# Weight tiles interleaved by columns with a step per stage, and two banks taken in turn, in a two-layer decoder trunk

## The reference, cut to what matters

```python
h = h + 0.5 * swiglu(rmsnorm(h, ffn1_norm[l]), ffn1_w_in[l], ffn1_w_out[l])
u = rmsnorm(h, mix_norm[l])
q_a, c_kv, iq, ik, iw, z_pool, q_c, gate_pre = jnp.split(u @ w_in[l], split_pts, axis=-1)
...
y_c = mem_attention(q_c, rmsnorm(mem, mem_norm[l]), w_mem_kv[l])
g = jax.nn.sigmoid(gate_pre).reshape(B, S, N_BRANCH, D)
merged = (g[:, :, 0] * (y_a @ w_branch_a[l])
          + g[:, :, 1] * (y_b @ w_branch_b[l])
          + g[:, :, 2] * (y_c @ w_branch_c[l]))
h = h + merged @ w_out[l]
h = h + 0.5 * swiglu(rmsnorm(h, ffn2_norm[l]), ffn2_w_in[l], ffn2_w_out[l])
```

## Time and profile before

| | |
|---|---|
| median of 3 runs | 2218.6 us (2218.0 to 2218.61) |
| the profiled execution's own time | 2218.74 us |
| its span in the trace | 2216.8 us |
| PE matmuls | 10264, busy 2200.5 us (99%) |
| PE weight loads | 10264, busy 1805.8 us (81%) |
| POOL busy | 1327.2 us (60%) |
| DVE busy | 932.4 us (42%) |
| ACT busy | 521.8 us (24%) |
| transfers | 209.72 MB, mean 95 GB/s |

### The profile page before, as it was taken

How to read it: one execution, slowest core, us unless ns; L and a number is a source line. 1 busy time by engine, 2 the same in 40 slices (tenths; PEclk the granted TensorE clock), 3 DMA queues, 4 the chain that set the end, 5 groups by cost and what they waited for, 6 DMA issues and landing times.

```text
span 2216.8 us, 30470 instructions
## 1 busy us (share of the span) xinstructions
PE 2200.5 (99%) x10264; PEld 1805.8 (81%) x10264; DVE 932.4 (42%) x1697; ACT 521.8 (24%) x1010; POOL 1327.2 (60%) x886
## 2 busy tenths in 40 slices
PE   9999999999999999999999999999999999999997
PEld 6888888878888888888888888887878888888886
DVE  5331345578854432023433213536887453320322
ACT  3110112443553211001111101125445432100111
POOL 7656657644446666665766666585444376656654
PEclk9999999999999999999999999999999999999999
DMA  5343323322213332332333332242222132323322
GB/s 185 95 138 103 101 76 115 104 67 63 71 53 101 96 101 82 104 100 86 96 109 126 105 106 95 81 129 85 63 72 67 48 114 95 95 88 106 100 76 85
DMA packets 68780, 209.72 MB, mean 95 GB/s; under 512 B 7600, under 2 KB 10840, under 8 KB 68440
## 3 DMA queue, kind: packets, MB, share of 16 engines
q1 hardware_dynamic: 64416, 203.10, 29.6%
q10 hardware_dynamic: 4280, 5.52, 0.8%
HBM read 206.48 MB, written 3.68 MB: 95 GB/s over the span
## 4 chain that ended last, share of the span: by engine, by line
PE 96%; DVE 2%; DMA 0%; issue 0%; ACT 0%; ACTq 0%; DVEq 0%
PE bank L613 30%; PE bank L614 29%; PE bank L615 29%; PE obank L866 2%; PE sbank L811 1%; PE tbank L833 1%; DMA h<-in_xT 0%; PE sbank L803 0%; DVE picks L1384 0%; PE sbank L764 0%; PE sbank L786 0%; PE sbank L817 0%; PE obank L850 0%; PE obank L624 0%; DVE top L1382 0%
## 5 line engine op out<-in xcount | busy, mean ns | idle before, releaser
L544 POOL TENSOR_TENSOR wL<-raw,wH 128x1024 fp32r<-128x1024 f32 (+3 forms) x424 | 894.2, 2109 | 35.4
L541 POOL TENSOR_SCALAR wH<-raw 128x1024 fp32r<-128x1024 f32 (+3 forms) x424 | 398.2, 939 | 818.6 <-PE bank L615 795.5
L613 PE MATMUL bank<-u0H,wH 128*128 128x512 f32 x1376 | 537.4, 391 | 0.0
L615 PE MATMUL bank<-u0L,wH 128*128 128x512 f32 x1376 | 535.4, 389 | 0.0
L614 PE MATMUL bank<-u0H,wL 128*128 128x512 f32 x1376 | 535.3, 389 | 0.0
L614 PEld LDWEIGHTS bank<-u0H,wL 128*128 128x128 f32 x1376 | 258.3, 188 | 54.5 <-issue 1.0
L613 PEld LDWEIGHTS bank<-u0H,wH 128*128 128x128 f32 x1376 | 258.3, 188 | 54.5 <-issue 1.0
L615 PEld LDWEIGHTS bank<-u0L,wH 128*128 128x128 f32 x1376 | 258.3, 188 | 53.6
L613 PE MATMUL bank<-u1H,wH 128*128 128x512 f32 x704 | 292.9, 416 | 0.0
L615 PE MATMUL bank<-u1L,wH 128*128 128x512 f32 x704 | 275.1, 391 | 0.0
L614 PE MATMUL bank<-u1H,wL 128*128 128x512 f32 x704 | 274.9, 390 | 0.0
(11 more groups left out here) (201 smaller groups left out, 2159.0 us busy)
## 6 DMA issues: line engine op xcount, KB each, us to landing
raw<-in_wA SPq DMA_DIRECT2D x176, 512.0 KB, 3.5
raw<-in_wM SPq DMA_DIRECT2D x96, 512.0 KB, 3.5
raw<-in_wB SPq DMA_DIRECT2D x64, 384.0 KB, 3.0
raw<-in_wB SPq DMA_DIRECT2D x64, 320.0 KB, 2.9
raw<-in_wR SPq DMA_DIRECT2D x32, 256.0 KB, 2.6
mem<-in_memT SPq DMA_DIRECT2D x2, 1024.0 KB, 6.6
near_bias<-bias_rows ACTq DMA_DIRECT2D x2, 1024.0 KB, 6.4
bias_rows<-bias_once ACTq DMA_DIRECT2D x1, 1536.0 KB
```

The source lines that it names most:

```text
L541: pool.tensor_scalar(wH[:, w, 0:cols], raw[:, slot, 0:cols], 1.0, 0.0, ALU.mult, ALU.add).then_inc(rounded, 1)
L544: pool.tensor_tensor(wL[:, w, 0:cols], raw[:, slot, 0:cols], wH[:, w, 0:cols].bitcast(F32), ALU.subtract).then_inc(split_done, 1)
L613: pe.matmul(dst, a, hi[:, k, :], start=first and i == 0, stop=False)
L615: mm = pe.matmul(dst, a, lo[:, k, :], start=False, stop=last and i == len(tiles) - 1)
```

## The change

It has two parts.

**Interleaving.** The host function `dealt` takes groups of `beside` tiles of a unit and puts their columns in turn: column n of tile t of the group comes to place n x `beside` + t. On the chip `tile_of` reads tile t back with a step of `beside` elements, so the weight load's pattern changes from 128 neighbouring elements of 4 bytes to 128 elements that lie `beside` elements apart. The numbers of transfers, of POOL's instructions, of matmuls and of weight loads, and their sizes, stay. The step is set for each stage:

| stage | matmuls in a layer | step, layer 0 | step, layer 1 |
|---|---|---|---|
| first block, `hidden` | 1056 | 4 | 2 |
| first block, `outs` | 528 | 6 and 5 | 1 |
| mixing block, `u1H`/`u1L` | 864 | 8 | 4 |
| `w_out` | 192 | 8 | 2 |
| second block, `hidden` | 1056 | 8 | 1 |
| second block, `outs` | 528 | 1 | 6 and 5 |

Keys, values and the branch units (`wR`) are not interleaved. With step 4 or 2 the first four tiles of a unit still fill its first half, as the two pieces of the first units ask.

**Values of the memory.** The loop over the two halves of the tokens, which was outermost, is now innermost: each of the three products is made for `bank[2]` and then for `bank[3]`.

```diff
+BESIDE_IN = ((4, 8), (2, 1))
+BESIDE_OUT = ((True, False), (False, True))
+BESIDE_MIX, BESIDE_WO = (8, 4), (8, 2)
...
+def dealt(unit, beside):
+    lead = unit.shape[:-1]
+    t = unit.reshape(*lead, -1, beside, P)
+    return np.swapaxes(t, -2, -1).reshape(*lead, -1)
...
+            def tile_of(rows, w, t, beside):
+                first = t // beside * beside
+                return rows[:, w, first * P:(first + beside) * P].rearrange(
+                    "p (n t) -> p t n", t=beside)[:, t - first, :]
+
-            def exact(dst, w, tiles, hi, lo, first=True, last=True, before=None, within=None):
+            def exact(dst, w, tiles, hi, lo, first=True, last=True, before=None, within=None, beside=1):
...
-                    a, b = wH[:, w, t * P:(t + 1) * P], wL[:, w, t * P:(t + 1) * P]
+                    a, b = tile_of(wH, w, t, beside), tile_of(wL, w, t, beside)
...
-                    a, b = wH[:, w, k * P:(k + 1) * P], wL[:, w, k * P:(k + 1) * P]
+                    a, b = tile_of(wH, w, k, beside), tile_of(wL, w, k, beside)
...
+                    beside_in, paired = BESIDE_IN[l][int(unit > 0)], BESIDE_OUT[l][int(unit > 0)]
...
+                                          beside=half if paired else 1
...
-                        for mb in range(2):
-                            rows = slice(mb * P, (mb + 1) * P)
-                            for t in range(4):
-                                k = 4 * (i - 2) + t
-                                a, b = wH[:, w, t * M:(t + 1) * M], wL[:, w, t * M:(t + 1) * M]
-                                dst = bank[2 + mb][:, 0:M]
+                        halves = [(bank[2 + mb][:, 0:M], slice(mb * P, (mb + 1) * P)) for mb in range(2)]
+                        for t in range(4):
+                            k = 4 * (i - 2) + t
+                            a, b = wH[:, w, t * M:(t + 1) * M], wL[:, w, t * M:(t + 1) * M]
+                            for dst, rows in halves:
                                 pe.matmul(dst, mem_hi[:, k, rows], a, start=k == 0, stop=False)
+                            for dst, rows in halves:
                                 pe.matmul(dst, mem_hi[:, k, rows], b, start=False, stop=False)
+                            for dst, rows in halves:
                                 mm = pe.matmul(dst, mem_lo[:, k, rows], a, start=False, stop=k == KD - 1)
...
+                              within=small_steps(PLAN[at]), beside=BESIDE_MIX[l]).then_inc(unit_used, 1)
...
+                          u1H, u1L, before=ready, beside=BESIDE_WO[l]).then_inc(unit_used, 1)
...
-            wA.append(t.reshape(2, FC, P, -1).transpose(1, 0, 2, 3).reshape(2 * FC, P, -1))
+            wA.append(dealt(t.reshape(2, FC, P, -1).transpose(1, 0, 2, 3).reshape(2 * FC, P, -1),
+                            BESIDE_IN[l][int(f == "ffn2")]))
...
-                dst.append(half.reshape(2 * KD, P, -1))
+                dst.append(dealt(half.reshape(2 * KD, P, -1), (y - x) // 2 if BESIDE_OUT[l][int(f == "ffn2")] else 1))
...
-        wM.append(cat([flat(tiles(w[:, c:c + P])) for c in cols]))
-        wM.append(flat(tiles(a["w_out"][l])))
+        wM.append(dealt(cat([flat(tiles(w[:, c:c + P])) for c in cols]), BESIDE_MIX[l]))
+        wM.append(dealt(flat(tiles(a["w_out"][l])), BESIDE_WO[l]))
```

More of the change, by code:

```diff
@@ L624, in mean_square, with rows_later @@
                 pe.matmul(obank[:, 0:cols], weights, src[:, 0:cols], start=True, stop=True).then_inc(norm_mean, 1)
-            def rows_later(dst, w, ready, high, low):
+            def rows_later(dst, w, ready, high, low, beside):
                 for k in range(KD):
@@ L637, in rows_later @@
                     low(k)
-                    mm = pe.matmul(dst, wH[:, w, k * P:(k + 1) * P], u0L[:, k, :], start=False, stop=k == KD - 1)
+                    mm = pe.matmul(dst, tile_of(wH, w, k, beside), u0L[:, k, :], start=False, stop=k == KD - 1)
                 return mm
@@ L664, in hidden @@
                                            lambda k: pe.wait_ge(u_high, l * 24 + (u_from + k + 1)),
-                                           lambda k: pe.wait_ge(u_ready, l * 24 + (u_from + k + 1))
+                                           lambda k: pe.wait_ge(u_ready, l * 24 + (u_from + k + 1)), beside_in
                                            ).then_inc(unit_used, 1)
@@ L668, in hidden @@
                             exact(bank[i][:, :], i, [(k, k) for k in range(KD)], u0H, u0L,
-                                  before=weights).then_inc(unit_used, 1)
+                                  before=weights, beside=beside_in).then_inc(unit_used, 1)
                             if first and i == 1:
@@ L689, in outs @@
                                     exact(bank[i][:, :], (2 * i + part_) % SPLIT_SLOTS, tiles, hidH, hidL, first=part_ == 0,
-                                          last=part_ == 1, before=ready).then_inc(unit_used, 1)
+                                          last=part_ == 1, before=ready,
+                                          beside=half if paired else 1
+                                          ).then_inc(unit_used, 1)
                     hidden(0, unit, chunk, True)
@@ L895, in _ @@
                               [(k, k) for k in range(KD)], u1H, u1L, before=ready,
-                              within=small_steps(PLAN[at])).then_inc(unit_used, 1)
+                              within=small_steps(PLAN[at]), beside=BESIDE_MIX[l]).then_inc(unit_used, 1)
                     else:
@@ L943, in _ @@
                     exact(bank[(C_WO + f) % BANKS][:, :], (U_WO + f) % SPLIT_SLOTS, [(k, k) for k in range(KD)],
-                          u1H, u1L, before=ready).then_inc(unit_used, 1)
+                          u1H, u1L, before=ready, beside=BESIDE_WO[l]).then_inc(unit_used, 1)
                 ffn(U_FFN2, C_FFN2, 16, 24, 5)
```

## The result

| | before | changed |
|---|---|---|
| median | 2218.61 us (4 runs, 2218.0 to 2219.06) | 2295.09 us (4 runs, 2295.02 to 2295.68) |
| span of the profiled execution | 2216.8 us | 2293.1 us |

The ratio is 1.0346, with a 95% interval of 1.0334 to 1.0358: the change makes the kernel 76.5 us slower. The time lies in the stated range, on the side that was given the larger chance, but nine times as far from 2218.6 as the 8.4 us of the forecast.

A forecast was written before the change was run, and what follows sets the result against it. PE's matmuls were taken as the bound: their number times their distance. Profiled span 2216.8 + 8.4 us for doubled loads behind short matmuls + 1.9 gave 2227.1, stated as 2227 us; range 2150 to 2300, the likeliest case's own 2222 to 2233.

The forecast's parts named there:

- What bounds the kernel: Whole kernel: PE's matmuls, busy 99% of the span; time is their number times their start-to-start distance, about 0.227 us.
- The values of the memory: 96 matmuls in both layers alternate between two banks: taken as 0, at most 0.9 us gain or loss.
- I take twice: Weight loads with a step of 4 or more: assumed to take twice as long, 213 ns instead of 107.
- The load behind short matmuls: Mixing block, both layers: doubled loads behind short or small matmuls lack cover and delay the next; 8.4 us in sum.
- A load of 213 under 512 columns is the same picture at twice the size, so 227 should stand.: Full 512-column streams: a doubled load stays hidden, the distance stays 227 ns, costing nothing.
- the rival of the outgrown cover: Strided loads under 512 columns: at three times the length, distance 320 + 4 ns, 494 us more, 2712 us; chance 0.06.
- The rest is thus a fixed amount for each matmul: All fp32r matmuls: about 13.4 ns beyond the columns' time, the same for 512 and 256 columns.
- the prediction's own sign: Profile after: prediction wrong if start distance differs between a stage with a step and one with step 1.
- Weaker forms: Strided stages: doubled load ends a few ns late, 3 ns x 5088 = 15 us; chance 0.11 shared with paid-for-each-fetch.
- The price for each fetch: Strided loads: each fetch stops the stream one column, 40 ns (step 2: 13.3), about 2447 us; chance 0.11 with weaker forms.
- The faster rival: Strided stages: the 13.4 ns are load reads clashing with the stream's, a step avoids it; down to 2149.5 us; chance 0.19.

The follow-up runs named there:

- mix_only: Changed kernel with interleaving undone in the four feed-forward blocks, kept in mixing block and w_out; 2250.04 us, ratio 1.0142 to the kernel before.
- twos: Changed kernel with step 2 for every step 4 and 8, step 1 in all outs; 2247.61 us, ratio 1.0131 to the kernel before.
- shifted: Kernel before, every step 1, with weight slots wH and wL moved 8 elements (32 bytes) on, activations left where they were; 2269.91 us, ratio 1.0233.
- shifted64: Kernel before, every step 1, with the weight slots moved 64 elements (256 bytes) on; 2218.83 us against 2218.3, ratio 1.0001.
- third grid: Separate kernel without the computation, timing matmuls on constant data with shifted operand starts and other stream lengths; no combination under 226.7 ns with 512 columns.

## Why the prediction was right and where it was wrong

*What bounds the kernel* was right, and so was what follows from it: PE's distances are the time, POOL and the transfers never came into it (the stages of `mix_only` add up to within 0.5 us).

*The values of the memory* at 0 were right: 120 ns in the trace, 2218.52 against 2218.33 us alone.

*"I take twice"* was right in kind. Loads with steps 4 to 8 take 0.33 us in the timeline where step 1 takes 0.19, 0.234 and 0.240 bare against 0.111: 2.1 to 2.2 times.

*The load behind short matmuls*, 8.4 us, was the right mechanism and nearly the right size: 6.1 + 4.7 = 10.8 us lie beside small matmuls, and the load there is 0.22 us from the next where 0.11 stood.

**The step that failed** is the term put at nothing: "A load of 213 under 512 columns is the same picture at twice the size, so 227 should stand." It measured 65 us (76.3 less 10.8 and the 0.3 at the start). Two things were wrong in it. First, a load does not need 213 ns but 234 to 240, and the text itself said that a load decides from about 220 ns on; the rival of the outgrown cover priced only three times, 2712 us, and passed over the values just above the edge. By the bare loads, as an estimate, 233.5 - 226.7 = 6.8 of step 4's 8.3 ns are the outgrown cover, and 239.7 - 226.7 = 13.0 of step 8's 18.0; what is over is not explained. The forecast was a step function near its edge, and a range of lengths belonged in it. Second, "The rest is thus a fixed amount for each matmul" was read from two lengths, 512 and 256, that happen to share it: 480 columns have some 17 ns and a shift by 32 bytes has 20. Step 2 lies there: a load of 118 ns with 109 to spare, and 6.6 ns for each matmul under 512 columns, 29 us in `twos`. By the prediction's own sign, a distance that differs between a stage with a step and one with step 1, its mechanism was wrong.

*The rivals.* The range held because of the sentence on "Weaker forms (a doubled load that ends a few ns late: 3 ns x 5088 = 15 us)": that is what steps 4 to 8 did, with 7 to 13 ns in place of 3. That 2295.1 us lies inside is in good part luck: the upper end, 2300, was set by halving a chance of 0.11 and not by a price, and the time is 5 us short of it. The price for each fetch, whose step 2 (13.3) and step 4 (40 ns) were both too dear, was refuted by `shifted`, which has the same fetches. The faster rival, a clash of two reads, came nearer to the mechanism that `shifted` shows, with the wrong sign. What was held against it, that `u0H` and `hidH` show the same 0.227, proves nothing: those tiles keep the same place against the weight slots modulo 256 bytes, as far as their sizes tell, and `shifted64` agrees. The kernel before already stood at the best place of those tried.

The Trainium skill (SBUF — State Buffer, section Door 1) says that at least two hits on a 16-byte line are needed for full bandwidth. The bare loads agree in the main: 118 ns with step 2, near the 111 of step 1, and 234 with step 4. Its other statement there, that one may stride over four float32 for free, does not hold for TensorE's moving operand in fp32r: with step 2, two hits on each line, the stream takes (407.87 - 386.13) / 48 = 0.453 us, twice its time. Nor does it hold for the load, with 234 ns at step 4. The measurement decides.

*What stays open*: by which rule the places work. Steps 12 (268.5 ns) and 24 (252.7) are dear and 16 and 32 (236.5, 236.3) cheap, 480 columns with step 4 take longer than 512, shifts of both reads by 8 and 16 are neutral and by 4 are not, and small matmuls between the large ones take part of the loss away (`twos`, `shifted`). Whether the 6.6 ns of step 2 are such a place or something of its own isn't settled: that they are gone under 480 columns and fewer speaks against a price of the load itself, one shift took half of them away, and none tried took all.

## What to carry to other kernels

Keep a stationary operand's columns next to each other: with a step of 16 or 32 bytes its load took twice the time, and under a stream of 512 fp32r columns that was just too long, while under full float32, a cover of 429 ns, it cost nothing. Where matmuls in a row start further apart than their columns explain, try the start addresses of the two SBUF operands against each other before anything else; here 32 bytes were worth 2.3% and 256 bytes nothing. And where a cost is zero up to an edge, work out how near the edge the case stands.

## What the runs showed of the hardware that was not expected

- 128 weights of 4 bytes load in 111 ns with step 1, 118 with step 2, 234 with step 4 and 240 with step 8, under 128 moving columns; the last two are the same at a granted clock of 0.50 and, under 256 columns, of 1.00 (233 and 241).
- Step 2 makes the distance 6.6 ns longer under 512 columns and no longer under 480, 384 and 256.
- The distance of fp32r matmuls over 512 columns goes from 226.7 to 236.6 ns by the start of the operands alone (236.6: the stream one element further, third grid). 504 columns take as long as 512 at the best place, 226.6 ns.
- Loading fewer columns (16 to 112) makes the distance longer, 229.0 to 235.6 ns, not shorter.
- A moving fp32r operand with step 2 takes 453 ns for 512 columns, twice the 227.
